# Order of the 512- and 256-column matmuls in the second unit of each merged pair

## The reference

```python
def swiglu(h, w_gu, w_down):
    gate, up = jnp.split(h @ w_gu, 2, axis=-1)
    return (jax.nn.silu(gate) * up) @ w_down

# first block, one layer
h = h + rmsnorm(m @ w_out, norm_mix_post)      # m: gated pool mixer and attention
a = jnp.square(jax.nn.relu(rmsnorm(h, norm_mlp_pre) @ w_up))
h = h + rmsnorm(a @ w_down, norm_mlp_post)
# second block, two layers
x = x + 0.5 * swiglu(rmsnorm_2(x, g_ffn1), w_ffn1_gu, w_ffn1_down)
z = rmsnorm_2(x, g_mix) @ w_mix_in             # conv b, c, v; attention q, k, v; forget gate
x = x + concat(rmsnorm_2(y_conv), rmsnorm_2(y_att)) @ w_mix_out
x = x + memory_cross_attention(rmsnorm_2(x, g_xattn), rmsnorm_2(mem, g_mem), w_xq, w_xkv, w_xo)
x = x + 0.5 * swiglu(rmsnorm_2(x, g_ffn2), w_ffn2_gu, w_ffn2_down)
```

## Time and profile before

| | |
|---|---|
| median of 3 runs | 1507.57 us (1507.49 to 1507.79) |
| the profiled execution | 1507.48 us |
| its span, first to last instruction | 1505.7 us |
| granted TensorE clock, mean | 0.999 of full |
| PE busy | 1495.8 us, 99% |
| weight loads (PEld), beside PE | 1288.3 us, 86% |
| DVE busy | 1020.7 us, 68% |
| ACT busy | 785.1 us, 52% |
| POOL busy | 54.7 us, 4% |
| from HBM | 277.49 MB, 186 GB/s over the span |
| chain that ended last | PE 93%, DVE 5%, ACT 1% |

### The profile page before, as it was taken

The page is one execution under the profiler, slowest core; times in us unless marked ns, Lnnn a source line. Parts: engine busy times, 40 slices in busy tenths (PEclk is TensorE's granted clock), DMA queues, the critical chain, the costliest instruction groups (busy, mean ns, idle before and its releaser), DMA issues.

```text
span 1505.7 us, 20960 instructions
## 1 busy us (share of the span) xinstructions
PE 1495.8 (99%) x8178; PEld 1288.3 (86%) x8178; DVE 1020.7 (68%) x1101; ACT 785.1 (52%) x899; POOL 54.7 (4%) x81
## 2 busy tenths in 40 slices
PE   9999999999999999999999999999999999999998
PEld 8878888888888888889888888888888888888886
DVE  5666766657566677987666667666567896676656
ACT  4554644446444465646544446444446655554444
POOL 0200100001000000010100001000000010000000
PEclk9999999999999999999999999999999999999999
DMA  9546455554555555353555455555545354355553
GB/s 375 201 146 246 168 190 184 184 195 168 195 191 175 213 197 175 141 195 112 196 190 189 179 195 196 199 191 195 191 172 200 137 195 168 112 196 195 188 191 124
DMA packets 40507, 280.44 MB, mean 186 GB/s; under 512 B 4608, under 2 KB 4864, under 8 KB 7040
## 3 DMA queue, kind: packets, MB, share of 16 engines
q1 hardware_dynamic: 39440, 275.08, 50.9%
q10 hardware_dynamic: 1008, 4.53, 0.8%
HBM read 277.49 MB, written 2.10 MB: 186 GB/s over the span
## 4 chain that ended last, share of the span: by engine, by line
PE 93%; DVE 5%; ACT 1%; issue 0%; DMA 0%; POOL 0%; SPq 0%; POOLq 0%; DVEq 0%; ACTq 0%
PE ps L399 90%; DVE w_lo L1514 2%; PE ps L624 1%; PE ps L616 1%; DVE accT L2014 0%; PE ps L666 0%; ACT Pb L1074 0%; DVE sT_lo L1521 0%; DMA raw<-stream_in 0%; DVE cu L2060 0%; DVE cu L2062 0%; ACT w_hi L1021 0%; DVE Pb L1547 0%; PE ps L970 0%; DVE Pb L1566 0%
## 5 line engine op out<-in xcount | busy, mean ns | idle before, releaser
L1514 DVE TENSOR_TENSOR w_lo<-raw,w_hi 128x2048 fp32r<-128x2048 f32 x250 | 571.5, 2290 | 256.0 <-ACT w_hi L1021 255.6
L1021 ACT ACTIVATE w_hi<-raw 128x2048 fp32r<-128x2048 f32 x251 | 479.8, 1914 | 291.2 <-PE ps L399 280.1
L399 PE MATMUL ps<-xT,w_hi 128*128 128x512 f32 (+1 forms) x2488 | 588.7, 378 | 0.0
L399 PEld LDWEIGHTS ps<-xT,w_hi 128*128 128x128 f32 x2488 | 444.5, 189 | 76.7 <-issue 0.2
L399 PE MATMUL ps<-xT,w_lo 128*128 128x256 f32 x2304 | 330.4, 282 | 0.0
L399 PEld LDWEIGHTS ps<-xT,w_lo 128*128 128x128 f32 x2304 | 314.9, 191 | 16.5
L399 PE MATMUL ps<-w_hi,sT_hi 128*128 128x512 f32 x576 | 186.2, 391 | 0.0
L399 PE MATMUL ps<-w_lo,sT_hi 128*128 128x512 f32 x576 | 185.5, 390 | 0.0
L399 PE MATMUL ps<-w_hi,sT_lo 128*128 128x512 f32 x576 | 185.3, 389 | 0.0
L399 PE MATMUL ps<-w_hi,xT 128*128 128x512 f32 x576 | 173.7, 392 | 1.3 <-ACT w_hi L1115 1.0
L399 PEld LDWEIGHTS ps<-w_hi,xT 128*128 128x128 f32 x576 | 107.7, 188 | 26.7 <-issue 3.2
(11 more groups left out here) (201 smaller groups left out, 932.0 us busy)
## 6 DMA issues: line engine op xcount, KB each, us to landing
raw<-stream_in SPq DMA_DIRECT2D x255, 1024.0 KB, 4.8
raw<-stream_in SPq DMA_DIRECT2D x4, 256.0 KB, 5.4
kTx<-mem_in SPq DMA_DIRECT2D x1, 1024.0 KB, 12.2
cu<-gate_bias_in SPq DMA_DIRECT2D x1, 1024.0 KB, 14.1
qk_tok<-post_gain_in ACTq DMA_DIRECT2D x1, 1024.0 KB, 5.2
kTx<-mem_in ACTq DMA_DIRECT2D x1, 1024.0 KB, 6.8
mem_kept<-kTx ACTq DMA_DIRECT2D x1, 1024.0 KB, 4.3
kTx<-mem_kept ACTq DMA_DIRECT2D x1, 1024.0 KB, 4.7
```

The costliest lines, as they stand in the source:

```text
L399: return nc.tensor.matmul(bank_ap, lh, rh, start=start, stop=stop)
L1021: nc.scalar.activation(w_hi[:, slot(c), 0:width], raw[:, slot(c), 0:width], copy).then_inc(unit_hi, 1)
L1514: nc.vector.tensor_tensor(w_lo[:, slot(c), :], raw[:, slot(c), :], w_hi[:, slot(c), :].bitcast(F32), sub).then_inc(unit_lo, 1)
```

## The change

In `merged`, `some` is split into `highs` (the 512-column matmuls, with the waits for free banks) and `lows` (the 256-column ones). The first unit calls both for all tiles, as before. The second unit calls `highs` for all four tiles, then `lows` for tiles 0 and 1, then the half signal and `between`, then `lows` for tiles 2 and 3: 16, 8, 8. Each matmul stays as it is.

```diff
-                def some(ks, fs):
+                def highs(ks, fs):
                     for f in fs:
...
+
+                def lows(ks, fs):
                     for k in ks:
                         kk = 4 * part + k
                         for f in fs:
...
-                    last = some(range(0 if tiles is None else 2, 4), range(4))
+                    ks = range(0 if tiles is None else 2, 4)
+                    highs(ks, range(4))
+                    last = lows(ks, range(4))
                 else:
                     if tiles is not None:
                         pe.wait_ge(turn_lo, tiles + BT)
+                    highs(range(4), range(4))
                     for fs in ((0, 1), (2, 3)):
-                        last = some(range(4), fs)
+                        last = lows(range(4), fs)
                         if fs[0] == 0 and half_sem is not None:
                             last.then_inc(half_sem, 1)
                         if fs[0] == 0 and between is not None:
```

## The result

The changed kernel takes **1510.14 us** (median of 20 runs, 1509.91 to 1510.50), the kernel before, run beside it, 1507.59 (20 runs, 1507.33 to 1507.86). The ratio is **1.0017**, with a 95% interval of 1.0010 to 1.0024: 2.5 us more, against a forecast of 2.4. The profiled execution has a span of 1508.2 us, the one before 1505.7. By the bound of 0.2% that the prediction set, this counts as no difference; over 20 runs a side it can just be told as slower. So the interest lies in the parts: a gain of 1.3 us and losses of 3.8 that a sum of 2.5 does not show.

The account below looks back on a forecast made before the run. PE, busy 1495.8 of 1505.7 us, was taken as the bound. Terms of -1.3, 0, +1.0, +2.5 and +0.1 gave +2.3 to +2.4, so 1507.48 + 2.4 = 1509.9 us, range 1508.2 to 1511.3.

Parts of the forecast that it names:

- the case called the likeliest: Whole kernel: time the same as before within 0.2%, chance 0.76.
- Term 1: PE's own time: one change from 256 to 512 columns fewer saves 0.02 us per second unit, -1.3 us in all.
- The count of 65: Second units credited with the 0.02 us gain: 70 less five whose time DVE sets.
- no gain from the order: Rival on PE's rhythm: the 0.03 us belongs to first matmuls after any break and stays; 1511.2 us, chance 0.07.
- Term 2: FFN blocks: the gate's sum comes 1.02 us later, hidden in the loop and at the FFN ends; cost 0.
- Three ends: 0: FFN ends: the hidden tile's rest still ready for PE with 0.05 us slack, so no cost at three ends.
- The rival was right in its mechanism: FFN ends do bind: lateness 0.1 us plus PE restart 0.1 at three ends, +0.6, 1510.5 us; chance 0.15.
- Term 3: Kernel's end: the never-used unit's residual on DVE delays the last additions, +1.0 us (0.8 to 1.1).
- Term 4: Cross-attention: head 0's later scores delay head 3's residual through DVE's queue, +1.26 us per layer, +2.5 in two.
- Nothing gives it back: Cross-attention: PE has no slack and later waits for DVE's division anyway, so the 1.26 us per layer stays lost.
- Term 5: Middle's convolution part, last pair: DVE's half-a sum starts 0.07 us later per layer, +0.1 in two (0 to 0.3).

Follow-up runs that it names:

- late_signal: Kernel before, old order 8, 8, 8, 8, with only the half signal and `between` moved behind the third run: 1511.46 us, ratio 1.0025.
- mixed: New order in 62 of 70 second units, old order in cross-attention's two, each FFN's last pair and each layer's last convolution pair: 1506.54 us, ratio 0.9993.
- x_old: Changed kernel with the old order back in each layer's second cross-attention query unit, new order in 68 of 70 units: 1507.84 us, ratio 1.0001.
- new_no_dead: Changed kernel without the two never-used units at the stream's end (no load, rounding or residual): 1509.95 us, ratio 1.0015.
- new_no_rest: Changed kernel without DVE's residual of the first never-used unit, loads and roundings kept: 1509.80 us, ratio 1.0014.
- scores_early: Changed kernel with cross-attention head 0's scores behind the first eight wide matmuls, ACT's, DVE's and PE's orders adapted: 1509.47 us, ratio 1.0013.
- last_block_only: New order only in the last gate/up pair of the kernel's last FFN, old order elsewhere: 1508.60 us, ratio 1.0006.
- x_new_only: New order only in each layer's second cross-attention query unit, old order elsewhere: 1510.00 us, ratio 1.0015.
- scores_late: Kernel before, old order and signals at their old places, only cross-attention head 0's scores moved behind the third run: 1509.95 us, ratio 1.0016.

## Why the prediction was right, and where its sizes were off

The forecast was 1509.9 us, the result 1510.14, inside the range of 1508.2 to 1511.3 and in the case called the likeliest (no difference beyond 0.2%). Step by step:

**Term 1, -0.02 per unit (-1.3).** Right: 5.586 became 5.566, and `late_signal` against the change prices it at 1.2 us in whole runs, `mixed` at 1.1; PE's starts sum to 1.31 over all 70 units. The count of 65 came out by luck: four of the five units left out gain too, and others in the middles give less than 0.02. The mechanism, as far as the runs go, is the change of width from 256 to 512 columns. The rival "no gain from the order" falls with `late_signal`: had the extra stayed, it and the change would take the same time. But its mechanism, slower first matmuls after any break, is seen as well, behind the late tiles of term 2; here the break itself was removed.

The Trainium skill (TensorE: Matmul & The Clock Gate, section Back-to-back issue gap) gives an isolated matmul a gap of its columns over 2.4 GHz plus about 2.5 ns; worked out from that formula, as estimates, 215.8 ns for 512 columns and 109.2 for 256, with no term for a neighbour. The matmuls here are not isolated, each has a weight load beside it, and the traces differ in both: 227 and 120 ns in long runs, and 233, 236, 228, 233, 231 behind a change of width.

**Term 2, the FFNs.** The sum of the gate moved by 1.04 (1.02 predicted), and the looped blocks hide it. The step that failed is the end of it, "Three ends: 0". The prediction took the matmul at 520.77 as the reader of the hidden tile and found a slack of 0.05. The first reader is that matmul's weight load, 0.22 earlier, so there was none: at each FFN end the load waits, PE is held for 0.03 to 0.04, and the next nine starts lose 0.04 more. That is 0.07 to 0.08 per end and 0.23 for the three, where 0 was forecast; the fourth, 0.07 again, delays PE's last matmul and not the kernel, whose end DVE sets. In `x_old`, `late_signal`, `new_no_dead`, `new_no_rest` and `scores_early`, which have the late signal at the FFN ends too, an end mostly costs 0.06 to 0.08 (0.04 to 0.10 in all); in the kernels whose signal stands at its old time there, `mixed` among them, it costs nothing. The rival was right in its mechanism, lateness and a restart, and too dear at 0.2 per end.

**Term 3, the very end (+1.0).** Right in place and size: +0.97 in the additions against PE's last matmul, and 0.9 in whole runs by `last_block_only`. What the prediction did not have is that the end is not simply additive behind it. With the rest taken away from the changed kernel the additions came 1.2 earlier against PE's last matmul, and the output's landing took 0.8 to 0.9 longer. Term 3 is a fact of the kernels that have the rest; the reverse, that removing the rest would win a microsecond, would have been wrong.

**Term 4, cross-attention (+1.26 per layer).** The mechanism is shown by three runs (`x_old`, `x_new_only`, `scores_late`), the size is 1.20. The predicted start of head 1's maximum was 1.26 later than before, and against the unit's start it came 1.22 later (703.90 - 694.05 against 703.01 - 694.38). The 0.04 is in the sum's 0.65: from its start to the maximum's it took 0.60 (703.30 to 703.90). Over the whole cross-attention PE lost 1.24 in layer 0 and 1.19 in layer 1, 2.43 where 2.52 was forecast. "Nothing gives it back" held in the changed kernel, and `scores_early` shows how near the next bound stands.

**Term 5, the convolution part (+0.07 per layer).** PE's step there grew by 0.088 and 0.095. The starts behind this stall are slower than 227 ns in the kernel before as well, and 0.04 less so in the changed one, so that 0.05 and 0.06 stay, 0.11 in all where 0.1 was forecast. As the earlier trace rows, ACT, DVE and PE:

```profile
628.51 0.60 ACT L1348 ACTIVATE qk_tok<-ps 128x512 f32<-128x512 f32 x1 [3.31 <-PE ps L399]
...
629.14 0.69 DVE L1965 TENSOR_TENSOR kTx<-ps,qk_tok 128x512 f32<-128x512 f32 x1
...
646.41 0.39 PE L399 MATMUL ps<-w_hi,xT 128*128 128x512 f32 x1
647.03 0.50 PE L399 MATMUL ps<-w_hi,xT 128*128 128x512 f32 x1 [0.23 <-DVE w_lo L1519]
```

ACT's copy ends last, at 629.11, and DVE's sum follows it. PE comes to the late weight rest at 647.03, with the wait named.

**The account.** Summed from PE's starts in the two traces: -1.31 (order) + 2.43 (cross-attention) + 0.11 (convolution part) + 0.30 (four FFN ends) + 0.04 (0.02 in the opening and some hundredths elsewhere) = 1.57, as measured at PE's last matmul. With 0.97 at the end that is 2.5, the difference of the spans. So the one term that was put at nothing, 0.30 at the FFN ends, was partly made up by cross-attention and the end, each a little smaller than forecast; that the total came within 0.3 us owes something to luck. Two traces alone would not settle sums this small: before the first merged pair they already differ by up to half a microsecond between kernels that are alike there, and by 0.04 in these two.

## What to carry to other kernels

A reordering that removes a switch in a full engine's stream also moves every signal inside it. Price both, the first per instance and the second at each reader, and expect the loss to sit in few places: here 60 units gained 0.02 each, two places lost 1.2 each, one lost 1.0, and each FFN end 0.07 to 0.08. Apply the order where the signal has slack, keep the old one where it has not (`mixed`), and where a slack works out at a few hundredths, ask for the first reader: here it was the weight load, 0.22 ahead of its matmul.

## What the runs showed that was not expected

**The extra behind a change of width is spread.** It is 0.027 us in all, over the first five 512-column matmuls behind 256-column ones (233, 236, 228, 233, 231 ns for 227), so runs of four pay 0.02. It isn't peculiar to a change of width: behind the late tile at an FFN's end, with 512 columns before and after, nine starts are 229, 234, 236, 224, 231, 235, 229, 232 and 231 apart. What the two have in common was not tested. The other way about there is a small gain: four narrow matmuls behind wide ones take 0.470 to 0.478 where four of 0.120 are 0.480.

**The landing of the last output.** 256 KB on ACT's queue took 2.9 us from issue to landing in ten kernels, the one before and the changed one among them, and 3.7 to 3.8 in the three whose last addition waited for PE, two of them without the unused loads and one with them. The DMA view of `new_no_dead` from 1503.4 on, just ahead of ACT's issue, has one packet on a queue other than the output's two:

```profile
q14 instruction: 1, 0.01, 0.2%
```

It is a packet of 8 KB on a queue that the view calls "instruction". It starts 2.1 to 2.2 us behind ACT's issue in all three kernels, and a few of the output's packets end up to 0.8 behind the rest. In the ten others the last such packet starts 1.9 ahead of ACT's issue, and none falls into the transfer. So the packet goes with the longer landing in 13 of 13 traces. No run moved it alone: that it is the cause is likely and not shown, and why it comes later in the three stays open.
